# 96 of 132 on-chip transposes of a ten-stage fp32 network moved from TensorE to transposing DMAs issued by ScalarE

## The reference

```python
def swiglu(h, w_gate, w_up, w_down):
    return (jax.nn.silu(h @ w_gate) * (h @ w_up)) @ w_down

for l in range(DEPTH):
    h = rms_norm(x, ffn1_norm[l])
    x = x + 0.5 * swiglu(h, ffn1_w_gate[l], ffn1_w_up[l], ffn1_w_down[l])
    h = rms_norm(x, mix_norm[l])
    ...
    h = rms_norm(x, ffn2_norm[l])
    x = x + 0.5 * swiglu(h, ffn2_w_gate[l], ffn2_w_up[l], ffn2_w_down[l])
```

## Time and profile before

| | |
|---|---|
| timed runs, median (range) | 1596.78 us (1595.99 to 1597.06) |
| profiled execution, span from first to last instruction | 1592.5 us |
| TensorE busy | 1577.1 us, 99% |
| VectorE busy | 1088.6 us, 68% |
| ScalarE busy | 879.6 us, 55% |
| granted TensorE clock, mean | 0.999 |

### The profile page before, as it was taken

The page is one execution under the profiler, slowest core; times in us unless marked ns, Lnnn a source line. Parts: engine busy times, 40 slices in busy tenths (PEclk is TensorE's granted clock), DMA queues, the critical chain, the costliest instruction groups (busy, mean ns, idle before and its releaser), DMA issues.

```text
span 1592.5 us, 21964 instructions
## 1 busy us (share of the span) xinstructions
PE 1577.1 (99%) x8000; PEld 1310.9 (82%) x8000; DVE 1088.6 (68%) x1884; ACT 879.6 (55%) x1760; POOL 97.7 (6%) x155
## 2 busy tenths in 40 slices
PE   9999999999999999999999999999999999999998
PEld 7888888788888888887788888998788889878886
DVE  6677788767767767678777767767654577575454
ACT  7444587744436434477764444776543477664442
POOL 1000022000000000011110000012000010110000
PEclk9999999999999999999999999999999999999999
DMA  9788844377877777783258876633665556156551
GB/s 350 260 309 291 240 161 141 98 271 261 278 269 196 268 271 259 257 212 107 89 207 272 287 268 216 212 120 127 207 197 184 170 178 236 35 199 221 183 186 52
DMA packets 97290, 332.14 MB, mean 209 GB/s; under 512 B 14625, under 2 KB 15393, under 8 KB 96673
## 3 DMA queue, kind: packets, MB, share of 16 engines
q1 hardware_dynamic: 78192, 277.65, 52.0%
q10 hardware_dynamic: 18992, 53.09, 10.4%
HBM read 329.64 MB, written 1.06 MB: 208 GB/s over the span
## 4 chain that ended last, share of the span: by engine, by line
PE 94%; DVE 2%; DMA 1%; ACT 1%; POOL 1%; issue 1%; SPq 0%; DVEq 0%; POOLq 0%; ACTq 0%
PE PS L976 27%; PE PS L978 26%; PE PS L977 26%; PE PS L1157 2%; PE PS L1054 2%; PE PS L1178 2%; PE PS L1220 1%; DMA raw<-in_ffn 1%; PE PS L1318 1%; PE PS L1319 1%; PE PS L1320 1%; PE PS L994 1%; PE PS L1200 1%; POOL st L2359 1%; PE PS L1255 0%
## 5 line engine op out<-in xcount | busy, mean ns | idle before, releaser
L1847 DVE TENSOR_TENSOR Wl<-raw,Wh 128x1024 fp32r<-128x1024 f32 (+3 forms) x360 | 354.7, 1030 | 27.1 <-ACT Wh L1456 26.1
L976 PE MATMUL PS<-Wh,Hh 128*128 128x512 f32 (+1 forms) x824 | 321.9, 391 | 1.7 <-DVE Hl L1907 1.7
L978 PE MATMUL PS<-Wh,Hl 128*128 128x512 f32 (+1 forms) x824 | 319.2, 387 | 0.0
L977 PE MATMUL PS<-Wl,Hh 128*128 128x512 f32 (+1 forms) x824 | 318.7, 387 | 0.0
L1456 ACT ACTIVATE Wh<-raw 128x1024 fp32r<-128x1024 f32 (+3 forms) x360 | 306.3, 903 | 21.7 <-PE PS L978 16.8
L1847 DVE TENSOR_TENSOR QTl<-raw,QTh 128x1024 fp32r<-128x1024 f32 (+3 forms) x236 | 231.6, 1020 | 17.6 <-ACT QTh L1456 17.0
L1541 ACT ACTIVATE WK<-PS,st 128x256 f32<-128x256 f32 x88 | 41.6, 473 | 333.6 <-PE PS L978 332.6
L976 PE MATMUL PS<-QTh,Hh 128*128 128x512 f32 (+2 forms) x536 | 209.0, 390 | 0.0
L978 PE MATMUL PS<-QTh,Hl 128*128 128x512 f32 (+2 forms) x536 | 206.6, 385 | 0.0
L1456 ACT ACTIVATE QTh<-raw 128x1024 fp32r<-128x1024 f32 (+3 forms) x236 | 200.5, 896 | 10.8 <-PE PS L978 10.1
L977 PE MATMUL PS<-QTl,Hh 128*128 128x512 f32 (+2 forms) x536 | 206.4, 385 | 0.0
(11 more groups left out here) (235 smaller groups left out, 2253.4 us busy)
## 6 DMA issues: line engine op xcount, KB each, us to landing
raw<-in_ffn SPq DMA_DIRECT2D x392, 512.0 KB, 5.4
BT<-in_ada ACTq DMA_DIRECT2D x96, 512.0 KB, 4.4
raw<-in_win SPq DMA_DIRECT2D x64, 512.0 KB, 5.1
raw<-in_wo SPq DMA_DIRECT2D x32, 512.0 KB, 5.4
raw<-in_win SPq DMA_DIRECT2D x8, 420.0 KB, 4.9
raw<-in_lat SPq DMA_DIRECT2D x6, 512.0 KB, 5.7
raw<-in_ffn SPq DMA_DIRECT2D x8, 256.0 KB, 5.7
BT<-in_nab SPq DMA_DIRECT2D x2, 1024.0 KB, 7.1
```

The costliest lines, as they stand in the source:

```text
L976: e.matmul(out_, xh, wh, start=start, stop=False)
L977: e.matmul(out_, xh, wl, start=False, stop=False)
L978: return e.matmul(out_, xl, wh, start=False, stop=stop)
L1847: ins = e.tensor_tensor(low(p)[:, cc], raw[p % RAW][:, cc], high(p)[:, cc].bitcast(f32), ALU.subtract)
```

## The change

For the groups g = 0 to 7 of each FFN (`by_dma`), which are 16 of its 22 tiles, TensorE issues nothing for `turn`. ScalarE gets a new event `pack` for each of these tiles, placed one event behind its `gu`. `pack` waits for the product, copies the tile as 16-bit halves with the two halves of each number separated, waits for its own copy, and issues a transposing DMA from SBUF to SBUF on its queue. `mend`, in the place of ScalarE's `turn`, waits for that DMA, puts the 16-bit halves together again into an fp32 tile (a second copy), waits for its own copy, and makes the high part from it. VectorE's part reads that tile in SBUF, not PSUM. The buffers lie in `QF`, which FFNs don't use. Groups 8 to 10 stay as they were.

```diff
+def by_dma(g):
+
+    return g < NG - 3
+
+
+def with_packs(ev):
+
+    out, due = [], None
+    for e in ev:
+        out.append(e)
+        if due:
+            out.append(due)
+            due = None
+        if e[0] == "gu" and by_dma(e[1]):
+            due = ("pack", e[1], e[2], 0)
+    return out
...
+    if kind == "f" and engine == "ACT":
+        ev = with_packs(ev)
...
             def turn(k, g, t):
-                z, n = ring_no[k, g, t], gu_no[k, g, t]
+                z, n = ring_at((k, g, t)), gu_no[k, g, t]
                 if z >= 2:
-                    e.wait_ge(f_z, z - 1)
+                    e.wait_ge(f_z, ring_no[ringed_turns[z - 2]] + 1)
                 e.wait_ge(f_mul, n + 1)
...
-                    elif what == "turn":
+                    elif what == "turn" and not by_dma(x):
                         turn(k, x, y)
...
+            def pack(k, g, t):
+
+                n, m = gu_no[k, g, t], cross_at((k, g, t))
+                e.wait_ge(f_mul, n + 1)
+                e.copy(packed(m).rearrange("p (h f) -> p h f", h=2),
+                       FA[:, n % 3, 1, :].bitcast(u16).rearrange("p (f h) -> p h f", h=2)).then_inc(f_pack, 1)
+                e.wait_ge(f_pack, m + 1)
+                e.dma_start_transpose(crossed(m).rearrange("p (b q) -> p b q", b=4), packed(m)).then_inc(f_cross[m % 4], 16)
+
+            def mend(k, g, t):
+
+                n, m, at = turn_no[k, g, t], cross_at((k, g, t)), mend_at((k, g, t))
+                e.wait_ge(f_cross[m % 4], 16 * (m // 4 + 1))
+                if at >= 2:
+                    e.wait_ge(f_z, cross_no[mended_turns[at - 2]] + 1)
+                own.mark(e.copy(mended(at).bitcast(u16).rearrange("p (q h) -> p h q", h=2),
+                                crossed(m).rearrange("p (h q) -> p h q", h=2)))
+                own.after()
+                e.activation(ATh[:, n % 4, :], mended(at), ACT.Copy).then_inc(f_hi, 1)
...
                     elif what == "turn":
-                        turn(k, x, y)
+                        (mend if by_dma(x) else turn)(k, x, y)
...
             def turn(k, g, t):
-                n, z = turn_no[k, g, t], ring_no[k, g, t]
+                n, turn_ = turn_no[k, g, t], (k, g, t)
+                src = mended(mend_at(turn_)) if by_dma(g) else PS[:, 6 + ring_at(turn_) % 2, 0:256]
                 e.wait_ge(f_hi, n + 1)
-                e.tensor_tensor(ATl[:, n % 4, :], PS[:, 6 + z % 2, 0:256], ATh[:, n % 4, :].bitcast(f32),
-                                ALU.subtract).then_inc(f_z, 1)
+                e.tensor_tensor(ATl[:, n % 4, :], src, ATh[:, n % 4, :].bitcast(f32), ALU.subtract).then_inc(f_z, 1)
```

More of the change, by code:

```diff
@@ L281, in walk @@
     ev = [e for e in ev if e]
+    if kind == "f" and engine == "ACT":
+        ev = with_packs(ev)
     return laid_end(s, engine, ev) if s in ENDS else ev
 def program(nc, d, out):
-    f32, f32r, i32 = mybir.dt.float32, mybir.dt.float32r, mybir.dt.int32
+    f32, f32r, i32, u16 = mybir.dt.float32, mybir.dt.float32r, mybir.dt.int32, mybir.dt.uint16
     ACT, ALU, AX = mybir.ActivationFunctionType, mybir.AluOpType, mybir.AxisListType
@@ L329, in program, with qf_slot, packed, crossed @@
         gates = [AT[:, part, 0, :] for part in range(2)]
+        def qf_slot(n):
+            return QF[:, n, :]
+        def packed(m):
+            return qf_slot(m % 4).bitcast(u16)
+        def crossed(m):
+            return qf_slot(4 + m % 4).bitcast(u16)
+        def mended(m):
+            return qf_slot(8 + m % 2)
         two = sb("two", [128, 4], f32r)
@@ L398, in program @@
             semaphore(n) for n in ("f_mm", "f_silu", "f_mul", "f_turn", "f_hi", "f_z"))
+        f_pack, f_cross = semaphore("f_pack"), [semaphore(f"f_cross{i}") for i in range(4)]
         ada_in = [semaphore(f"ada_in{i}") for i in range(2)]
@@ L548, in weights_to @@
             for s in range(len(STAGES)):
+                at = -1
                 for i, ev in enumerate(order[s]):
                     top = n
-                    if ev[0] == "parts":
+                    at += ev[0] != "pack"
+                    if ev[0] == "pack":
+                        pass
+                    elif ev[0] == "parts":
                         top = max(n, 2 * min(NP, first[STAGES[s]] + ev[1]) + ev[2])
@@ L556, in weights_to @@
                         laid = s in ENDS and i >= end_at(order[s])
-                        goal = (0, 12, 16, 16, 16, 18)[i] if s == 0 and i < 6 else n if laid else n + 2 * room(ev)
-                        while top < min(2 * NP, goal) and slot_free[top // 2] <= freed_before[s, i] + own:
+                        goal = (0, 12, 16, 16, 16, 18)[at] if s == 0 and at < 6 else n if laid else n + 2 * room(ev)
+                        while top < min(2 * NP, goal) and slot_free[top // 2] <= freed_before[s, at] + own:
                             top += 2
@@ L564, in program @@
         act_weights, dve_weights = weights_to(ACT_WALK), weights_to(DVE_WALK)
-        gu_no, gu_kept, turn_no, down_no, ring_no, gu_in = {}, {}, {}, {}, {}, {}
+        gu_no, gu_kept, turn_no, down_no, gu_in = {}, {}, {}, {}, {}
+        cross_no, ring_no = {}, {}
         for s, (kind, k) in enumerate(STAGES):
@@ L579, in program, with cross_at, mend_at, ring_at @@
                     turn_no[k, x, y] = len(turn_no)
-                    ring_no[k, x, y] = len(ring_no)
+                    (cross_no if by_dma(x) else ring_no)[k, x, y] = turn_no[k, x, y]
                 elif what == "down" and 1 in z:
                     down_no[k, x, y] = len(down_no)
+        crossed_turns, mended_turns, ringed_turns = [t for t in gu_no if by_dma(t[1])], list(cross_no), list(ring_no)
+        def cross_at(turn):
+            return crossed_turns.index(turn)
+        def mend_at(turn):
+            return mended_turns.index(turn)
+        def ring_at(turn):
+            return ringed_turns.index(turn)
         def gu_bank(n):
@@ L1050, in turn @@
                     e.wait_ge(id_in, 16)
-                elif z == 1:
-                    e.wait_ge(f_mul, 3)
                 for c in range(2):
@@ L1057, in down @@
             def down(s, i, k, g, t, chunks):
-                n, z = turn_no[k, g, t] % 4, ring_no[k, g, t]
-                e.wait_ge(f_z, z + 1)
+                n = turn_no[k, g, t] % 4
+                e.wait_ge(f_z, turn_no[k, g, t] + 1)
                 for x in chunks:
@@ L1549, in gate @@
                                 allow_slow_non_contiguous=True).then_inc(mod_out, 16)
+            def pack(k, g, t):
[14 more added lines that the diff above has]
+                e.activation(ATh[:, n % 4, :], mended(at), ACT.Copy).then_inc(f_hi, 1)
             def turn(k, g, t):
-                n, z = turn_no[k, g, t], ring_no[k, g, t]
-                e.wait_ge(f_turn, n + 1)
+                n, z = turn_no[k, g, t], ring_at((k, g, t))
+                e.wait_ge(f_turn, z + 1)
                 e.activation(ATh[:, n % 4, :], PS[:, 6 + z % 2, 0:256], ACT.Copy).then_inc(f_hi, 1)
@@ L1781, in act_program @@
                                 triangle()
+                    elif what == "pack":
+                        pack(k, x, y)
                     elif what == "turn":
-                        turn(k, x, y)
+                        (mend if by_dma(x) else turn)(k, x, y)
                         if s == y == 0 and x == 1:
```

## The result

The changed kernel is slower: 1617.16 us in the median of four runs (1611.42 to 1624.47) against 1596.92 us of the kernel before on the same chip, a measured ratio of 1.0136, 95% interval 1.0119 to 1.0154 (the two medians by themselves give 1.0127). The prediction said 1589.2 us and 0.48 for faster; the time lies inside its range and on the other side of no change. The profiled execution took 1611.42 us, its span is 1609.6, against 1592.5 before.

What follows compares the result with a forecast made beforehand. TensorE's queue of matmuls without gaps bounds the kernel; -22.1 + 7.2 + 6.6 + 0.7 = -7.6 us takes the span from 1592.5 to 1584.9, with 4.3 for the median 1589.2 us. Range 1579 to 1655; 0.48 for faster.

Steps and rivals of the forecast that it cites:

- the price of the issue: ScalarE, each of the 96 tiles: issuing the transposing DMA takes 0.33 us, the median issue on this queue.
- the DMA loop: Rival, chance 0.34: above a 6.4 us landing, ScalarE's mend waits in 84 tiles; 1626 us at 6.8, 1868 at 9.5.
- What is removed: TensorE's queue: 96 transpose pairs at 0.23 us each go, 22.1 us off.
- The middle of an FFN: Transfers stay hidden up to a landing of 6.4 us; silu distance falls from 8.45 to 8.22 us.
- L: Time from a transposing DMA's issue to its landing: taken as 5.7 us, between bounds of 2.0 and 12.3.
- the issue is long: Rival, chance 0.12: issue on ScalarE's queue takes 1.1 us, +6 to 1595 us; at 2 us, +13 to 1602.
- The starts of stages 2, 3 and 5: `down(0,1)` waits 2.4 us for the low part behind its DMA's landing and mend; three stages, 7.2 us.
- Stages 7 and 9: Second block: 3.3 us lost in each, from `down(0,1)` and the second token tile's input; 6.6 us for both.
- the input of the second token tile: Stages 7 and 9: two packings delay the making of this input, by 1.0 and 0.9 us.
- `down(0,1)` (1.4): Stages 7 and 9: TensorE ready at 1130.78, low part at 1132.15 after its DMA's landing, a 1.4 us wait.
- Stage 0: Same order as stage 7 without the second token tile's input: half of 1.4, so 0.7 us lost.
- Span to median: Timed median taken to lie 4.3 us above the profiled span, turning 1584.9 into 1589.2 us.

Runs made afterwards that it cites:

- experiment 8: Changed kernel with only g 2 to 7 through transposing transfers, issued by SyncE instead of ScalarE: 1584.88 us, 0.9933 of the kernel before.
- experiment 11: Kernel with g 2 to 7, plus ScalarE repeating one copy 11 times in the first pair of stages 2, 3 and 5: 1589.87 us, 0.9971.
- experiment 9: Changed kernel with only g 1 to 7 through transposing transfers, g 0 back on TensorE: 1584.8 us, 0.9933 of the kernel before.
- experiment 10: Changed kernel with g 2 to 8 through transposing transfers, the other groups on TensorE: 1583.22 us, 0.9936 of the kernel before.
- experiment 1: Changed kernel with only g 2 to 7 through transposing transfers, g 0 and 1 back on TensorE: 1579.77 us, 0.9903 of the kernel before.
- experiment 12: Kernel with g 2 to 7 through transposing transfers on ScalarE's queue, measured once more without an edit: 1577.91 us, 0.9886 of the kernel before.
- experiment 3: Changed kernel plus useless TensorE matmuls ahead of the waiting `down` at the starts of stages 0, 2, 3 and 5: 1613.83 us, 1.0109.
- experiment 4: Changed kernel with all 96 transposing transfers issued by SyncE's queue, ScalarE only packing: 1596.74 us, 1.0011 of the kernel before.
- experiment 6: Changed kernel with no transfer at all, the mend reading the packed tile (output differs): 1578.45 us, 0.9895 of the kernel before.
- experiment 5: Changed kernel with plain copies of the same bytes in place of transposing transfers (output differs): 1599.79 us, 1.0029 of the kernel before.
- experiment 2: Changed kernel with only g 0 and 1 through transposing transfers, the rest back on TensorE: 1630.15 us, 1.0217 of the kernel before.

## Why the prediction was wrong

The forecast of a gain failed at four places: the price of the issue, the path that the first tiles take, one landing time for the whole program, and a clock that had no term. The time lies inside the range by luck: the range reached so high only for the DMA loop, which cost some 3 us in this kernel, and without it the mechanisms that the prediction priced end at 1602.

- **What is removed** (22.1 us): right. In the trace with g 2 to 7 the last lag of -15.2 is made of -1.7 ahead of 20 us, +3.4 of more idle time of TensorE behind that and so -16.9 for 72 pairs, 0.235 each against 0.23: 22.5 us for 96.
- **The middle of an FFN** (hidden up to L = 6.4): right. Silu distance 8.17 us against 8.22; L 4.2 in the median. But it was close: in the middle of stages 2, 3 and 5 short landings of 2.4 to 4.6 us and long ones of 5.3 to 6.4 follow each other in turn. In three tiles behind the starts L was 8.5, 8.2 and 7.8 (issued at 118, 1158 and 1457), the mend waited 2.63, 1.75 and 1.31 us, and TensorE then 1.67, 0.68 and 0.81: the rival with the DMA loop, in three tiles out of 84. It came in experiment 8 too.
- **The price of the issue** (0.33 us): this is the step that failed first. The instruction took 1.21 us and held ScalarE 1.34. I took it from loads on the same queue and gave the long one 0.12. Even the plain copy within SBUF took 0.47. The rival "the issue is long" had the mechanism and the size (1.1 us), and its sum was still too low, +6 to 1595, for the two reasons below and because it counted only 0.8 us more at each start of 2, 3 and 5.
- **The starts of stages 2, 3 and 5** (2.4 us each): measured 3.8, and for another reason. I let `down(0,1)` wait for the landing. In the trace the mend waits for nothing; the chain runs through ScalarE's four weight copies, VectorE's splits of them and the product of (1,1), which stand ahead of the low part. With the assumed kind of issue (plain, 0.60 us of stall) the wait is 2.30: the number of the prediction came out, its cause did not, as L = 5.7 was not what made it: that agreement is luck. VectorE's queue was left out of this step of the working.
- **Stages 7 and 9** (3.3 us each): 5.5 in stage 7 as the sum of four waits, less the 0.87 us that stood there before, and 4.8 in stage 9; 2.6 and 2.9 with plain transfers, 1.0 without any. For the input of the second token tile (1.9) the mechanism was right and the issue mis-sized: 3.2. For `down(0,1)` (1.4) the number came near, 1.67, and the cause was again another. Its transfer, issued at 1139.90, landed after 2.4 us, the mend at 1145.28 waited for nothing, and VectorE's four weight splits, 1142.30 to 1146.93, stood ahead of the low part as in stage 2. The fourth wait, 0.68 at 1173, belongs to the landing of 8.2 us above. PE at stage 7 in the changed kernel:

```profile
1130.68 0.47 PE L1032 MATMUL PS<-Wh,Hh 128*128 128x512 f32 x1 [2.86 <-DVE Hl L1983]
1134.85 0.47 PE L1032 MATMUL PS<-Wh,Hh 128*128 128x512 f32 x1 [1.17 <-DVE Hl L1983]
1147.65 0.50 PE L1032 MATMUL PS<-QTh,AT 128*128 128x512 f32 x1 [1.67 <-DVE AT L2025]
```

- **Stage 0** (0.7 us): measured 8.1 us in its first holes (1.7 at 25, 6.4 at 37). One value of L was used for the whole program, 5.7; the row that had 9.5 us for a load on this queue was in front of me, and in stage 0, with the weight buffers being filled, the first transfer took 9.1. The 1.7 at 25 are the issue: ScalarE stood idle for 1.42 us behind it, ahead of the next silu. Moreover 1.7 us came at 133, behind a transfer that landed after 8.5 us:

```profile
126.46 0.77 ACT L1620 COPY QF<-QF 128x512 uint16<-128x512 uint16 x1 [2.63 <-DMA QF<-QF]
```

Its issue took 2.16 us, right after two other loads on ScalarE's queue, but the hole goes with the landing: for the tile at this place in experiments 11, 9, 10, 1 and 12 L was 7.5, 8.1, 8.5, 9.1 and 11.0 us and the hole 0.6, 1.3, 1.8, 2.2 and 4.4, and in experiment 12 that issue took 1.23. The hole at 37 shrinks to 3.5 with plain transfers and to 1.1 without any.
- **The clock** (no term): the sum had none. There are six falls, 23.9 us at half speed. Some 3.9 us of that lie within the holes themselves (3.4 in stage 0, 0.5 in stage 3), where TensorE had nothing to slow down; the other 20.0 cost some 8.8 us at the 1.5 us per 3.4 that experiment 11 shows. One of the six, at 788, lies in a mixer, behind waits that the kernel before has too. This is an addition from the trace, and experiment 3 shows that it can't be had back simply by filling the holes at four of the places.
- **Span to median** (+4.3): the changed kernel's median lies 7.6 us above its span. Its runs spread over 13 us, those of before in that set over 1.3; with the spread goes the mean granted clock, 0.992 in the fastest and 0.984 to 0.985 in the two slowest.

The terms once more for the profiled span, +17.1 us: -22.5 removed; +11.3 for the starts of 2, 3 and 5; +10.3 for stages 7 and 9 (5.5, and 2.3 + 1.7 + 0.8); +9.8 for stage 0; +8.8 for the clock. That is +17.7. The changed kernel's trace is 1.6 us ahead before its first transfer, at 20 us, which leaves 16.1 of the 17.1. That lead isn't the change's work: its matmuls stood 0.23 us apart from 6.4 us on, those of the trace before from 10.3 on. The kernel with g 2 to 7 has such a lead too, 1.7 us at 20 us.

The Trainium skill (DMA: Bandwidth & Descriptors, Why a DMA increments its semaphore by 16 and not by 1) led to an estimate of 1.1 us for the issue at 32 tiles; the 1.21 us of the trace are near it. But its price by the tile isn't borne out here: a transfer of half the tiles took 1.27 us, where that estimate would have 0.7.

The Trainium skill (VectorE: DVE Perf Modes, Rules for kernel authors) prefers TensorE wherever PSUM will do as the destination. For g 0, 1 and 8 the runs agree (1.0217 with g 0 and 1 alone; adding 8 took more than it gave); for g 2 to 7 they don't (0.9903 and 0.9886), where TensorE is the bound and ScalarE has 1.3 us to stand still.

What stays open: what decides whether the granted clock falls. Holes of 2.7 us had a fall behind them in two places and none in the third of one trace; at the starts of stages 2, 3 and 5 those of 0.97 to 1.16 us had none (experiments 4, 6, 9) and those of 2.3 to 3.8 in experiment 5 and the changed kernel all had one; the 2.86 us above, in stage 7, had none here and one in experiments 2 and 3; and in the mixers the same pair of waits, 0.59 and 1.20 us, stands in every kernel and has a fall behind it in some. The kernel before has runs with falls too: in the set of experiment 1 its mean granted clock was 1.000 in the fastest (1592.75 us) and 0.995 in the slowest (1600.84). Why the landing at 110 to 118 us varies from 7.5 to 11.0 us on the same queue is open as well; the fastest kernel still has the hole that it makes.

## What to carry to other kernels

Work taken off the bounding engine and given to a helper pays only where the helper has room in every one of its stretches. Cost the start and the end of each loop by themselves, along all queues that the late item passes (here VectorE's), and with the worst landing of the trace where the loads crowd, not the median. And give the issue of a DMA of a new kind a range of its own: it is time of the engine that issues it, and two issues of half the width cost here twice as much as one. When two traces are compared, start behind the point from which both run at the full clock. Then apply the change by group: the same edit was +2.2% on g 0 and 1 and -1.0 to -1.1% on g 2 to 7.
